# Expert gates: a table filled by one-hot products, and the same table filled by adding DMAs

## The reference, cut to what matters

```python
# 512 tokens, D = 1024, 8 heads, 128 x 128 = 16384 experts, 16 chosen by each head
q = (xb @ w_q).reshape(block, 8, 2, 128)
s = jnp.einsum('thjd,hjkd->thjk', q, sub_keys)          # two scores of 128 keys a head
sv, si = lax.top_k(s, 16)
cand = sv[:, :, 0, :, None] + sv[:, :, 1, None, :]      # 16 x 16 pairs
cs, ci = lax.top_k(cand.reshape(block, 8, 256), 16)
eidx = i1 * 128 + i2                                    # i1, i2: the two keys of a pair
g = softmax(cs)
act = gelu(einsum('td,thkd->thk', xb, expert_u[eidx]))
out = einsum('thk,thkd->td', g * act, expert_v[eidx])
```

## Time and profile before

| | |
|---|---|
| median of three runs | 4669.53 us (4669.34 to 4669.65) |
| the profiled execution, span from first to last instruction | 4667.2 us |
| between that span and the median of the runs | 2.3 us |
| TensorE / VectorE / ScalarE / POOL busy | 95% / 54% / 31% / 7% |
| mean granted TensorE clock | 0.981 of full |

### The profile page before, as it was taken

One profiled execution on the slowest core, in us unless ns is written; L12 is line 12 of the kernel. 1 busy time (PEld: TensorE's weight loads), 2 busy tenths in 40 slices (PEclk: granted clock), 3 DMA queues, 4 the chain that ended last, 5 costly groups with the idle time before them and its releaser, 6 DMA issues. The chain is left out here.

```text
span 4667.2 us, 58760 instructions
## 1 busy us (share of the span) xinstructions
PE 4455.6 (95%) x22068; PEld 3726.6 (80%) x22068; DVE 2500.4 (54%) x3598; ACT 1454.4 (31%) x1579; POOL 306.1 (7%) x178
## 2 busy tenths in 40 slices
PE   8999889999999999989998999899999999999997
PEld 7888658888887778878996887777778888888886
DVE  4333444334335743346777343478888884555554
ACT  3222443222223532223443122233333332222221
POOL 0000000000000000001111000000000001333331
PEclk9999989999999999989999999999999999999998
DMA  3232102223322133222211232345545566565553
GB/s 118 96 90 85 37 29 88 99 88 101 99 89 73 28 91 99 84 72 64 63 59 52 85 98 85 115 131 138 137 128 176 180 193 216 189 198 191 191 193 108
DMA packets 514507, 519.84 MB, mean 111 GB/s; under 512 B 41173, under 2 KB 475469, under 8 KB 513374
## 3 DMA queue, kind: packets, MB, share of 16 engines
q1 hardware_dynamic: 514398, 518.41, 36.4%
HBM read 444.94 MB, written 73.40 MB: 111 GB/s over the span
## 5 line engine op out<-in xcount | busy, mean ns | idle before, releaser
L78 DVE TENSOR_TENSOR w_lo<-w_raw,w_hi 128x2048 fp32r<-128x2048 f32 (+2 forms) x326 | 667.8, 2050 | 919.4 <-ACT w_hi L72 919.3
L72 ACT CAST w_hi<-w_raw 128x2048 fp32r<-128x2048 f32 (+2 forms) x326 | 557.6, 1713 | 1259.1 <-PE psum L3119 491.5
L94 PE MATMUL psum<-h_hi,w_hi 128*128 128x512 f32 x1552 | 612.5, 395 | 16.3 <-DVE w_lo L78 13.3
L96 PE MATMUL psum<-h_hi,w_lo 128*128 128x512 f32 x1552 | 607.6, 391 | 0.0
L95 PE MATMUL psum<-h_lo,w_hi 128*128 128x512 f32 x1552 | 607.5, 391 | 0.0
L94 PE MATMUL psum<-h_hi_peer,w_hi 128*128 128x512 f32 x1104 | 437.6, 396 | 23.9 <-DVE w_lo L2966 16.1
L96 PE MATMUL psum<-h_hi_peer,w_lo 128*128 128x512 f32 x1104 | 431.2, 391 | 0.0
L95 PE MATMUL psum<-h_lo_peer,w_hi 128*128 128x512 f32 x1104 | 430.8, 390 | 0.0
L3117 PE MATMUL psum<-pr_act_hi,w_hi 128*128 128x512 f32 x1024 | 398.3, 389 | 0.0
L3118 PE MATMUL psum<-pr_act_lo,w_hi 128*128 128x512 f32 x1024 | 398.3, 389 | 0.0
L3119 PE MATMUL psum<-pr_act_hi,w_lo 128*128 128x512 f32 x1024 | 398.3, 389 | 0.0
(11 more groups left out here) (467 smaller groups left out, 7432.2 us busy)
## 6 DMA issues: line engine op xcount, KB each, us to landing
w_raw<-in_ffn_w_gate_up_dram SPq DMA_DIRECT2D x176, 512.0 KB, 4.2
w_raw<-in_peer_u_dram SPq DMA_DIRECT2D x256, 256.0 KB, 5.1
w_raw<-in_peer_v_dram SPq DMA_DIRECT2D x128, 512.0 KB, 4.2
w_raw<-in_w_in_dram SPq DMA_DIRECT2D x64, 512.0 KB, 4.3
peer_hidden<-pr_q SPq DMA_DIRECT2D x64, 512.0 KB, 4.0
peer_gates<-pr_staged SPq DMA_DIRECT2D x8, 4096.0 KB, 12.9
pr_back<-peer_hidden SPq DMA_DIRECT2D x64, 512.0 KB, 6.2
pr_gate<-peer_gates SPq DMA_DIRECT2D x64, 512.0 KB, 7.2
```

The costliest lines, as they stand in the source:

```text
L72: c.nc.scalar.copy(c.hi[:, slot, :cols], c.raw[:, slot, :cols]).then_inc(c.hi_ready, 1)
L78: c.nc.vector.tensor_tensor(c.lo[:, slot, :cols], c.raw[:, slot, :cols], c.hi[:, slot, :cols].bitcast(F32), ALU.subtract).then_inc(c.lo_re ...
L94: c.nc.tensor.matmul(out, w_hi, x_hi, start=(n == 0), stop=False)
L96: mm = c.nc.tensor.matmul(out, w_lo, x_hi, start=False, stop=(n == last))
```

## The change

The table `gates` is laid out anew, [KEYS, P, T]: first key, second key, token. It is cleared during `sb_attention`, by 16 DMAs of 2 MB on SP's queue from a tile of zeros. VectorE no longer builds one-hot matrices; `finish` computes for each chosen pair its place in the table, (i1 x 128 + i2) x 512 + token, as an unsigned integer. POOL issues, for each head, 4 x 16 = 64 indirect DMAs. Each takes 128 shares and 128 places (one of each in every partition, that is, for 128 tokens) and adds each share, 4 bytes, to the table in DRAM. Before the next head's it waits for all earlier ones, because two heads of one token may choose the same expert. The spreading and the transposes of the choices are gone from all engines, and SP waits for all 512 DMAs where it waited for the stores of the table.

```diff
@@ sb_attention @@
+        zeros = sb("zeros", [P, P])
+        cleared = c.gates.rearrange("a p t -> (a p t)").rearrange("(n p x u) -> n p x u", p=P, x=CLEAR_ROWS * TC, u=P)
             with sp.Fori(0, SB_GROUPS) as i:
                 for j in range(2):
                     load_tile(c, sp, uq + i, j, wide_parts(c, j, w_in, i * 256 + j * D))
+                sp.wait_ge(zeroed, 1)
+                for q in range(GATE_CLEARS // SB_GROUPS):
+                    sp.dma_start(cleared[bass.ds(i * (GATE_CLEARS // SB_GROUPS) + q, 1)].rearrange("n p x u -> p (n x) u"),
+                                 zeros[:, :].unsqueeze(1).broadcast_to([P, CLEAR_ROWS * TC, P])
+                                 ).then_inc(c.gates_cleared, 16)
             following(sp)
+            sp.wait_ge(c.gates_cleared, 16 * GATE_CLEARS)
+            pool.memset(zeros[:, :], 0.0).then_inc(zeroed, 1)
@@ peer, sync: the hidden stage is one loop; store_gates is gone @@
                 if n == UNITS - 3:
-                    for p in range(2):
-                        sp.wait_ge(written[p], 16 * SPREAD_ROUNDS * ROUND_GROUPS // 2 + 16)
+                    sp.wait_ge(scattered, 16 * NH * PICKS)
                     for m in range(2):
                         sp.wait_ge(stored[m], 32)
                         fetch(m, m)
@@ peer, gpsimd @@
+            pool.iota(token[:, :], pattern=[[P, TC]], base=0, channel_multiplier=1,
+                      allow_small_or_imprecise_dtypes=True).then_inc(numbered, 1)
+            pool.wait_ge(c.gates_cleared, 16 * GATE_CLEARS)
+            for n in range(NH):
+                pool.wait_ge(placed, n + 1)
+                if n:
+                    pool.wait_ge(scattered, 16 * n * PICKS)
+                for t in range(TC):
+                    for k in range(n * TOP, (n + 1) * TOP):
+                        pool.indirect_dma_start(
+                            out=table, out_offset=bass.IndirectOffsetOnAxis(ap=place[:, t, k:k + 1], axis=0),
+                            in_=share[:, t, k:k + 1], in_offset=None, compute_op=ALU.add).then_inc(scattered, 16)
@@ peer, vector, finish: build is gone @@
-                step(V.tensor_tensor(rows[:, 2, :, n * TOP:(n + 1) * TOP], weight[:, :, :],
+                of_head = slice(n * TOP, (n + 1) * TOP)
+                step(V.tensor_tensor(share[:, :, of_head], weight[:, :, :],
                                      total[:, 0:TC].unsqueeze(2).broadcast_to([P, TC, TOP]), ALU.mult))
+                step(V.scalar_tensor_tensor(spot[:, :, :], key[:, 0], float(KEYS), key[:, 1], ALU.mult, ALU.add))
+                step(V.scalar_tensor_tensor(spot[:, :, :], spot[:, :, :], float(T),
+                                            token[:, :].unsqueeze(2).broadcast_to([P, TC, TOP]), ALU.mult, ALU.add))
+                V.tensor_copy(place[:, :, of_head], spot[:, :, :]).then_inc(placed, 1)
@@ peer, scalar: take_chosen and stage are gone; the hidden stage is units only @@
@@ peer, tensor: turn_rows and spread_quads are gone @@
-            with pe.Fori(1, CHOSEN_AT // 2) as i:
+            with pe.Fori(1, UNITS // 2) as i:
                 hide(uA + i, 0, i * 2)
                 hide(uA + i, 1, i * 2 + 1)
-            at = uA + CHOSEN_AT // 2
-            hide(at, 0, CHOSEN_AT)
-            pe.wait_ge(steps, count_of_steps())
             pe.wait_ge(s_taken, NH)
-            turn_rows(0)
...
```

More of the change, by code:

```diff
@@ L2548 @@
 EARLY = 8
[L2549 to L2572, removed]
+RANKED_AT = NH * PIECES - EARLY
+PICKS = TC * TOP
 def peer(c, gain, w_q, sub_keys, u, v, h, hidden, gates, h_rows):
@@ L2584, in peer @@
         q = sb("q", [P, 2, 2, T])
-        chosen = sb("chosen", [P, 3, T])
+        share = sb("share", [P, TC, SLOTS])
+        place = sb("place", [P, TC, SLOTS], U32)
+        token = sb("token", [P, TC])
         with ExitStack() as pre_ph:
@@ L2604, in peer @@
             total = sb("total", [P, 8], on=pre_ph)
[L2605 to L2609, removed]
+            key = sb("key", [P, 2, TC, TOP], on=pre_ph)
+            spot = sb("spot", [P, TC, TOP], on=pre_ph)
         act_hi = sb("act_hi", [P, 2, 2, T], F32R)
@@ L2612, in peer @@
         back = sb("back", [P, 2, 2, T])
-        gate = sb("gate", [P, 2, N_TG, 2, TG])
+        gate = sb("gate", [P, 2, 2, T])
         prod = sb("prod", [P, 2, 2, T])
-        keys_loaded, stored, written, hid_loaded, gate_loaded = (
-            [sem(c, f"pr_{n}{j}") for j in range(2)] for n in (
-                "keys_loaded", "stored", "written", "hid_loaded", "gate_loaded"))
+        keys_loaded, stored, hid_loaded, gate_loaded = (
+            [sem(c, f"pr_{n}{j}") for j in range(2)] for n in ("keys_loaded", "stored", "hid_loaded", "gate_loaded"))
         h_free = sem(c, "pr_h_free")
         h_stored, h_back = c.rows_loaded[0], c.rows_loaded[1:3]
-        (q_taken, keys_turned, keys_taken, scored, s_taken, indexed, steps, shifted, weighed, rows_turned,
-         chosen_taken, turned, gelued, built, spread, taken, gated, hi_done, lo_done, added) = (
+        (q_taken, keys_turned, keys_taken, scored, s_taken, indexed, steps, shifted, weighed, numbered, placed,
+         scattered, turned, gelued, gated, hi_done, lo_done, added) = (
              sem(c, f"pr_{n}") for n in (
                  "q_taken", "keys_turned", "keys_taken", "scored", "s_taken", "indexed", "steps",
-                 "shifted", "weighed", "rows_turned", "chosen_taken", "turned", "gelued", "built", "spread", "taken",
-                 "gated", "hi_done", "lo_done", "added"))
+                 "shifted", "weighed", "numbered", "placed", "scattered", "turned", "gelued", "gated", "hi_done",
+                 "lo_done", "added"))
+        table = gates.rearrange("a p t -> (a p t)").unsqueeze(1)
         ps = c.psum
@@ L2997, in _ @@
             turned_lo(0)
-            for n in range(CHOSEN_AT):
+            for n in range(RANKED_AT):
                 turn(n + 1)
@@ L3087, in hide @@
                 hide_half(j, 1).then_inc(c.tile_used, 1)
-            def turn_rows(r):
-                if r >= 2:
-                    pe.wait_ge(chosen_taken, r - 1)
-                for t in range(TC):
-                    mm = nc.tensor.transpose(ps[:, 6 + r % 2, t * P:(t + 1) * P], rows[:, r, t, :], c.ident[:, :])
-                mm.then_inc(rows_turned, 1)
-            def spread_quads(o, quads):
-                for k in quads:
-                    pe.wait_ge(built, o * ROUND_QUADS + k + 1)
-                    pe.wait_ge(taken, o * ROUND_QUADS + k + 1)
-                    for t in range(QUAD):
-                        mm = nc.tensor.matmul(ps[:, 6 + k % 2, t * KEYS:(t + 1) * KEYS], second[:, k % RING, t, :],
-                                              first[:, k % RING, t, :], start=True, stop=True)
-                    mm.then_inc(spread, 1)
             def outputs(use, j, m, begin, end):
@@ L3123, in _ @@
             pe.sem_inc(scored, 2)
-            pe.sem_inc(spread, RING)
-            pe.sem_inc(taken, 2)
             pe.sem_inc(gelued, 2)
```

149 lines of the change are left out of this document (38 added, 111 removed).

## The result

The changed kernel takes 4909.4 us (median; 4908.5 to 4912.1), the kernel before, on the same chip, 4669.4 (4668.8 to 4669.7). The ratio is 1.052 with a 95% interval of [1.050, 1.053]: slower by 240 us. The span of the profiled execution is 4906.8 us, the mean granted clock 0.947 where it was 0.981. The time lies outside the range; what happened is rival A.

What follows compares the result with a forecast made beforehand. TensorE, busy 95% of the span, was taken as the bound. -126.2 (products and transposes) + 4.5 (VectorE) + 0 (clears) + 0 (POOL) = -121.7 us, giving 4548 us; range 4535 to 4760.

Steps and rivals of the forecast that it cites:

- rival A: POOL's adding DMAs too dear, at SP's wait before the first fetches: (d - 1.38) x 512, 4865 at d = 2.0; chance 0.27.
- d: Price of one of POOL's 512 adding DMAs, estimated at 1.2 us, between 0.37 and 2.2.
- break-even of 1.62: Price of one POOL DMA, 1.62 us, at which the change was reckoned to be worth nothing.
- The chain: POOL's 512 adding DMAs, from head 0's placing at about 3071.4; predicted done at 3703, 92 us before anyone waits.
- the free distance of 1.38: POOL's price for each of 512 DMAs, 1.38 us, up to which SP's wait at 3795 costs nothing.
- The landing: Wait for a head's DMAs to land before the next head's: eight of 2.2 us, from the smallest DMA's median.
- The products and transposes gone: Spreading products and transposes off TensorE's queue, units 33 to 63 at 10.88 us each: gain 126.2 us.
- VectorE's added work: Three more small operations a head in the ranking, about 0.75 us; six heads exposed, 4.5 us added.
- The clears: 16 clears of 2 MB on SP's queue in the attention layer, ahead of the next weights: 0 to 2 us, taken as 0.
- rival D: Clears hold up the attention's weights: at 128 GB/s +10 to 40 us, 4560 to 4590; chance 0.03.
- Rival C: VectorE's two-input operations delayed behind POOL's issues while heads are ranked: +35 us, 4583; chance 0.11.
- The Trainium skill's price: About 2.0 us plus bytes for a POOL-issued DMA, mostly write receipt; taken for each of the 512, 4865 us.

Runs made afterwards that it cites:

- heads4: `aligned` with the adding DMAs of only the first four heads (256 instead of 512): 4548.2 us.
- heads6: `aligned` with the adding DMAs of only the first six heads (384 instead of 512): 4644.7 us, ratio 0.995.
- plain: `aligned` with the same 512 DMAs writing instead of adding, so some shares are lost: 4569.1 us; timed again in rounds 4568.0 us, ratio 0.979.
- before_odd: The kernel before with one unused tile of 16 bytes a partition ahead of the output products' tiles: 4689.0 us against 4668.5, ratio 1.0042.
- aligned: The changed kernel with `token` padded from 16 to 512 bytes a partition: 4892.1 us, ratio 1.048.
- merged: `aligned` with writing DMAs in head order; VectorE adds earlier heads' shares of equal pairs beforehand, full computation: 4593.5 us against 4668.2, ratio 0.985.
- half: `aligned` with 64 partitions a DMA instead of 128, so half the tokens get no gates: 4789.1 us.

## Why the prediction was wrong, point by point

**The failed step is the value of d.** "I put it somewhat above: d = 1.2 us" was taken from POOL's 128x4 operation (1.01 us). Measured: 2.03 us. Of it, 0.95 is a plain issue, 0.59 the addition, 0.30 the time between two issues, 0.13 the lengthening beside VectorE, and some 0.05 the twelve longer gaps. The nearest row by engine and size was no neighbour by kind. The same section had the upper end at 2.2, so the true value lay inside the bounds and near the far one. With a value known only between 0.37 and 2.2, and a break-even of 1.62 close to its upper third, 0.27 for rival A and a range cut at d = 1.8 were too narrow: d = 2.2 gives 4548 + 420 = 4968, and this end belonged into the range.

**The frame around it was right.** The chain starts at 3071.4 as worked out; the place (SP's wait ahead of the fetches), the free distance of 1.38 and the factor of 512 give 341 us for a measured 339.8. The landing was taken at 2.2 us and the waits were 3.4 on the mean (8 us). heads4 and heads6 show the flat part and the slope.

**The products and transposes gone: right.** Unit 63 ends at 3813.3, "about 3815" was predicted, and the units come at the distance of the undisturbed ones of the earlier trace rows. ScalarE's GELUs of after:

```profile
3476.14 1.03 ACT L2773 ACTIVATE pr_q<-psum 128x1024 f32<-128x1024 f32 x1 [6.54 <-PE psum L96]
...
3791.58 1.03 ACT L2773 ACTIVATE pr_q<-psum 128x1024 f32<-128x1024 f32 x1 [6.53 <-PE psum L96]
```

315.44 us for 29 units, 10.88 each. VectorE's added work costs 12 matmuls in the ranking (1574 instead of the 1586 of the earlier trace rows), 3 us where 4.5 were summed.

**The clears: right, rival D wrong.** SP's queue and ScalarE's uses of the weights, which answer to the earlier trace rows:

```profile
418.02 19.93 SPq L946 DMA_DIRECT2D peer_gates<-sb_zeros  x4
438.60 7.84 SPq L65 DMA_DIRECT2D w_raw<-in_sb_w_in_dram  x4
...
474.13 3.68 ACT L72 CAST w_hi<-w_raw 128x2048 fp32r<-128x2048 f32 x2
...
534.97 3.68 ACT L72 CAST w_hi<-w_raw 128x2048 fp32r<-128x2048 f32 x2
```

474.13 and 534.97, where before shows 474.08 and 533.67; the two later groups are 0.3 and 1.4 us behind before. All of it is inside the 0 to 2 of the prediction.

**Rival C had the right pair and the wrong victim.** VectorE's subtractions stay at 1218 ns (1217 before). It is POOL's issue that is longer beside them, by 0.9 us in the rows above and up to 2.2, 68 us over all 512; and it is longer only where the VectorE instruction had started first. Where POOL had started first, neither is, with one exception in 66 (89 subtractions began beside a running issue, and they take 1.22 us on the mean like the others). In after every one of these microseconds is on the path. The Trainium skill's "SBUF — State Buffer", section "Who interferes with whom", lets a VectorE instruction with two SBUF inputs contend with a POOL instruction that reads SBUF; by that rule an indirect issue is such a reader, and the traces agree about the pair, for adding issues and for writing ones (0.95 us, up to 2.76 in plain).

**The term that was missing** is the place of tiles in memory: 16 bytes of `token`, 20 us in the output phase (20.5 in before_odd). I listed the new tiles' instructions and not the addresses that they shift.

**The Trainium skill's price.** The Trainium skill's "DMA: Bandwidth & Descriptors", section "Anatomy of one DMA — SWDGE (gpsimd) path", puts a POOL-issued DMA at about 2.0 us plus bytes and most of it into the receipt. Taken as the price of each, it gave 4865, close to the 4892 of aligned. The trace doesn't agree with the reason: issues of one head follow each other without waiting for a landing, at 1.26 us in plain and 1.85 in after, while the wait for a landing is 3.3 and 3.4 us on the mean. The number was near by coincidence, but it was a warning worth more than the 0.27 that it got.

## What to carry to other kernels

Where a change issues hundreds of small DMAs, work out first the distance at which they become free and at which they are worth nothing, and if no row shows the instruction itself, let the range reach to its upper bound; bytes say nothing here, since an undisturbed issue of 512 bytes cost POOL 1.26 us when it wrote and 1.85 when it added, and half the bytes saved 0.14. If the addition at the destination is what makes it dear, an engine with room can do it beforehand, as merged does. And look at what a new small tile does to the addresses of the tiles allocated behind it: an unused one can cost 3% of a matmul-bound phase.

## What the runs showed of the hardware

- An indirect DMA from POOL, one 4-byte element for each of 128 partitions: 0.95 us busy and 0.30 to the next when it writes, 1.545 and 0.30 when it adds; with 64 partitions 1.40 instead of 1.545. Packets a DMA: 32 writing, 144 adding, 80 adding with 64 partitions.
- Between adding issues of 128 partitions a gap is longer by 1.4 to 4.6 us at every 60th and every 113th; in plain and half only at every 113th (four gaps each).
- Adding and writing ones take about equally long to land: 3.4 and 3.3 us of waiting between heads on the mean (2.1 to 5.3, and 1.9 to 4.7).
- With the activation tiles (not the weights) 16 or 32 bytes off their place, matmuls of 512 float32r columns follow each other every 0.2333 us instead of 0.2267, at the full granted clock; a shift of 512 bytes has no such effect.
- POOL's indirect issues that start while a two-input VectorE instruction runs are lengthened (78 of 82, up to 3.73 us instead of 1.545), those that start before it are not (65 of 66), and the 128x1024 subtractions never are (1218 ns, 1217 without POOL).
- During the hole the granted clock stands at 0.50, that is 1.2 GHz of 2.4, with TensorE idle; the first nine matmuls from 4153.1 on take 0.77 and 0.63 us, and from 4157.4 on they take 0.40, at a granted clock of 1.00.
- 2 MB of zeros in runs of 512 bytes, four such DMAs in a row, land in a median of 15.5 us after their issue.
